# An MoE layer with four experts of 32 slots at a time instead of two of 64, gate and up weights loaded by quarters of the contraction

## The reference, cut to what matters

```python
g_idx = jnp.argmax(g_logits, axis=-1)                 # one group of four
e_val, e_idx = lax.top_k(e_in_group, TOP_K_IN_GROUP)  # two of its eight experts
combine = jnp.sum(jax.nn.one_hot(expert_id, N_EXPERTS) * e_w[..., None], axis=1)
a = jnp.einsum('nd,edh->neh', t, w_gate)
b = jnp.einsum('nd,edh->neh', t, w_up)
act = jax.nn.silu(a) * b * combine[:, :, None]
out = jnp.einsum('neh,ehd->nd', act, w_down)
```

## Time and profile before

| | us |
|---|---|
| median of 3 runs (lowest, highest) | 1275.25 (1270.68, 1278.07) |
| the profiled execution | 1280.37 |
| its span | 1278.5 |
| experts of layer 0: first `gate_up` to end of the last `down` | 314.9 to 626.5 |
| experts of layer 1: first transposes of a round to end of the last `down` | 969.8 to 1239.2 |

### The profile page before, as it was taken

The page is one execution under the profiler, slowest core; times in us unless marked ns, Lnnn a source line. Parts: engine busy times, 40 slices in busy tenths (PEclk is TensorE's granted clock), DMA queues, the critical chain, the costliest instruction groups (busy, mean ns, idle before and its releaser), DMA issues.

```text
span 1278.5 us, 14637 instructions
## 1 busy us (share of the span) xinstructions
PE 1089.1 (85%) x5429; PEld 574.4 (45%) x5429; DVE 476.8 (37%) x1014; ACT 257.0 (20%) x498; POOL 185.4 (15%) x209
## 2 busy tenths in 40 slices
PE   5799888987999789999879999989765988878864
PEld 3344555555444234443345565658662422222223
DVE  3355556234233113332263336784540111111116
ACT  2211334022333123223231110000221000000001
POOL 1020000002322023221100002130011222222100
PEclk8899989986999899999889999999967989889997
DMA  9996985532899569999870200505320899999943
GB/s 351 404 322 264 251 294 225 227 132 70 313 395 401 228 238 356 398 406 410 305 286 1 99 1 0 230 1 198 154 94 20 325 413 413 413 412 407 407 161 129
DMA packets 94241, 324.54 MB, mean 254 GB/s; under 512 B 17647, under 2 KB 33423, under 8 KB 77380
## 3 DMA queue, kind: packets, MB, share of 16 engines
q1 hardware_dynamic: 71936, 303.49, 61.3%
q0 software_dynamic: 15504, 13.37, 3.4%
q10 hardware_dynamic: 6708, 6.45, 1.4%
HBM read 333.22 MB, written 30.11 MB: 284 GB/s over the span
## 4 chain that ended last, share of the span: by engine, by line
PE 63%; DMA 19%; DVE 7%; issue 4%; ACT 3%; SPq 3%; POOL 0%; ACTq 0%; another core or an unknown queue 0%; POOLq 0%; DVEq 0%
PE bank L849 15%; DMA ring<-in_moe_w_up 10%; PE bank L997 10%; PE bank L863 6%; PE bank L668 3%; PE bank L1036 3%; PE bank L784 3%; DMA ring<-in_w_ada 3%; DMA hT<-in_hy_log_decay 3%; PE bank L564 3%; PE bank L599 2%; PE bank L1025 2%; PE bank L983 2%; DMA ring<-in_moe_w_down 2%; PE bank L796 2%
## 5 line engine op out<-in xcount | busy, mean ns | idle before, releaser
L849 PE MATMUL bank<-ring,work 128*64 128x512 f32 x1120 | 267.5, 633 | 44.3 <-issue 38.2
L849 PEld LDWEIGHTS bank<-ring,work 128*64 128x64 f32 x1120 | 82.5, 145 | 220.6 <-issue 216.4
L863 PE MATMUL bank<-ring,work 128*64 128x512 f32 x560 | 129.4, 604 | 4.3 <-DVE work L1643 1.5
L997 PE MATMUL bank<-hT,ring 128*128 128x384 f32 x384 | 128.0, 494 | 5.3 <-ACT hT L1134 5.3
L1655 DVE SCALAR_TENSOR_TENSOR work<-bank,work 128x256 f32<-128x256 f32 x32 | 15.5, 484 | 261.3 <-ACT work L1230 248.6
L997 PEld LDWEIGHTS bank<-hT,ring 128*128 128x128 f32 x384 | 74.0, 194 | 58.0 <-issue 9.7
L863 PEld LDWEIGHTS bank<-ring,work 128*64 128x64 f32 x560 | 37.5, 138 | 74.1 <-issue 63.4
L1230 ACT ACTIVATE work<-bank 128x256 f32<-128x256 f32 x32 | 12.3, 383 | 249.8 <-PE bank L849 249.8
L1667 DVE COPY work<-bank 128x512 f32<-128x512 f32 x32 | 22.1, 692 | 106.8 <-PE bank L863 106.8
L1806 POOL DMA_INDIRECT work<-token_vectors,work x28 | 28.7, 1026 | 199.6 <-PE bank L832 185.7
L564 PE MATMUL bank<-ring,condS 128*32 128x256 f32 x768 | 48.6, 408 | 10.0 <-DVE ada L1334 5.5
(11 more groups left out here) (269 smaller groups left out, 1481.5 us busy)
## 6 DMA issues: line engine op xcount, KB each, us to landing
ring<-in_moe_w_gate SPq DMA_DIRECT2D x32, 2048.0 KB
ring<-in_moe_w_up SPq DMA_DIRECT2D x32, 2048.0 KB
ring<-in_moe_w_down SPq DMA_DIRECT2D x32, 2048.0 KB
ring<-in_w_ada SPq DMA_DIRECT2D x24, 2048.0 KB, 12.5
ring<-in_hy_w_in SPq DMA_DIRECT2D x6, 2048.0 KB, 20.4
filter_spectra<-work ACTq DMA_DIRECT2D x8, 768.0 KB
work<-expert_rows SPq DMA_DIRECT2D x16, 384.0 KB, 6.7
ring<-filter_spectra SPq DMA_DIRECT2D x2, 3072.0 KB, 12.1
```

Source lines behind the costliest of these rows:

```text
L849: last = mm(bank[2][WIN * j:WIN * (j + 1), :], gt[:, k, WIN * j:WIN * (j + 1)], gu[:, :, j, k, :], start=(k == 0), stop=(k == KD - 1))
L863: last = mm(bank[b + hf][WIN * j:WIN * (j + 1), :], AT[:, k, WIN * j:WIN * (j + 1)], dn[:, j, k, hf * HALF:(hf + 1) * HALF], start=(k == 0 ...
L997: last = mm(bank[n % 2][:, 0:T], w[:, k, (n % 4) * P:(n % 4 + 1) * P], hT[:, k, :], start=(k == 0), stop=(k == KD - 1))
```

## The change

The unit becomes a quad: four consecutive experts of 32 slots each (`QUAD` = 4, `WIN` = 32, 8 rounds). `gate_up` is 32 products of 32 slots by 512 columns (64 instructions), four experts in four quarters of the array's columns; `down` is 16 products (32 instructions). Further windows are of 32 slots per expert: up to two per quad are woven into the round (`extra_gate_up` behind the quad's own `gate_up`, `extra_down` behind its `down`), and `rare(q)` takes any beyond two.

A quad's weights fill the whole ring in six units of 2 MB. Units 0 to 3 hold a quarter of the contraction of gate and up for all four experts (two transfers of 1 MB each, contiguous pieces of 2 KB), units 4 and 5 the two halves of down. Units 0 to 3 of the next quad are issued when the activation of this one has been transposed (`at_mm`), so after its further windows' `gate_up` too; units 4 and 5 when the next quad's tokens have been transposed (`gt_mm`), so after `down`.

```diff
-PAIRS = NE // 2
-WIN = 64
+QUAD = 4
+QUADS = NE // QUAD
+WIN = P // QUAD
+WOVEN = 2
...
+        def load_unit(sp, l, q, i):
+
+            if i < 4:
+                cols = slice(i * (KD // 4) * EH, (i + 1) * (KD // 4) * EH)
+                for u, name in enumerate(("moe_w_gate", "moe_w_up")):
+                    src = a[name][l, QUAD * q:QUAD * (q + 1)].rearrange("j (p k) h -> p j (k h)", p=P)
+                    sp.dma_start(part_gu(i)[:, u].rearrange("p j k h -> p j (k h)"), src[:, :, cols])\
+                        .then_inc(sem(f"part_in{i}"), 16)
...
-            for q in range(2, PAIRS):
-                sp.wait_ge(S_("gu_mm"), B_("gu_mm") + q - 1)
-                load_gu(sp, l, q)
-                sp.wait_ge(S_("dn_mm"), B_("dn_mm") + 2 * (q - 1))
-                load_dn(sp, l, q)
-                if l == 0 and q % 2 == 1:
-                    load_filter(sp, q // 2)
+            for q in range(1, QUADS):
+                sp.wait_ge(S_("at_mm"), B_("at_mm") + q)
+                for i in range(4):
+                    load_unit(sp, l, q, i)
+                sp.wait_ge(S_("gt_mm"), B_("gt_mm") + 2 * (q + 1))
+                if l == 0:
+                    load_filter(sp, q)
+                for i in (4, 5):
+                    load_unit(sp, l, q, i)
...
-                for q in range(PAIRS):
-                    s = q % 2
-                    pe.wait_ge(sem(f"gu_in_{s}"), B_("gu_in") + 32 * (q // 2 + 1))
-                    copied(q)
+                for q in range(QUADS):
+                    pe.wait_ge(S_("gta_set"), B_("gta_set") + q + 1)
+                    pe.wait_ge(S_("gtb_set"), B_("gtb_set") + q + 1)
                     if q >= 1:
                         pe.wait_ge(S_("act_set"), B_("act_set") + q)
-                    extra(q)
-                    gate_up(GT, s, S_("gu_mm"))
...
+                    rare(q)
+                    apart(pe)
+                    for i in range(2):
+                        pe.wait_ge(sem(f"part_in{i}"), B_("part_in0") + 32 * (q + 1))
+                        gate_up(GT, i)
+                    if l == 0 and q >= 1:
+                        for part in range(3):
+                            spectra(q - 1, part)
+                    for i in range(2, 4):
+                        pe.wait_ge(sem(f"part_in{i}"), B_("part_in0") + 32 * (q + 1))
+                        last = gate_up(GT, i)
+                    last.then_inc(S_("gu_mm"), 1)
+                    extra_gate_up(q)
                     pe.wait_ge(S_("act_set"), B_("act_set") + q + 1)
-                    turn_act(S_("at_mm"))
...
+                    turn_act(A, S_("at_mm"))
+                    if l == 0:
+                        taps(q, 0)
+                        taps(q, 1)
                     pe.wait_ge(S_("at_set"), B_("at_set") + q + 1)
-                    pe.wait_ge(sem(f"dn_in_{s}"), B_("dn_in") + 16 * (q // 2 + 1))
+                    pe.wait_ge(sem("dn_in"), B_("dn_in") + 32 * (q + 1))
                     if q >= 1:
                         pe.wait_ge(S_("y_set"), B_("y_set") + 2 * q)
-                    down(s, 4, S_("dn_mm"))
...
+                    for hf in range(2):
+                        down(hf).then_inc(S_("dn_mm"), 1)
+                    if l == 0:
+                        taps(q, 2)
+                    extra_down(q)
+                    if q + 1 < QUADS:
+                        pe.wait_ge(S_("gath"), B_("gath") + 16 * (q + 1))
+                        for half in range(2):
+                            gather_turn(half)
+                    if l == 0 and q >= 1:
+                        sizes(q - 1)
```

More of the change, by code:

```diff
@@ L326, in build @@
         mtmp = [small(2, TC, NE) for _ in range(3)]
-        posk, rowk, wck, basek, wink, rowq = [small(2, TC) for _ in range(6)]
+        posk, rowk, wck, basek, wink = [small(2, TC) for _ in range(5)]
         idx = sb("idx", [P, TC * 2], I32)
@@ new lines, in gate_up_all, with turn_act, down @@
+                def gate_up_all(gt):
+                    for i in range(4):
+                        last = gate_up(gt, i)
+                    return last
+                def turn_act(act, done):
+                    for k in range(2):
+                        last = tr(bank[3][:, k * P:(k + 1) * P], act[:, k * P:(k + 1) * P], ident)
+                    last.then_inc(done, 1)
+                def down(hf):
+                    for k in range(2):
+                        for j in range(QUAD):
+                            last = mm(bank[4 + hf][WIN * j:WIN * (j + 1), :], AT[:, k, WIN * j:WIN * (j + 1)],
+                                      unit_dn(k)[:, j, hf * HALF:(hf + 1) * HALF], start=(k == 0), stop=(k == 1))
+                    return last
@@ L1650, in moe @@
                 dve.wait_ge(S_("tab_in"), B_("tab_in") + 16)
[L1651 to L1653 removed]
+                for q in range(QUADS):
+                    rare(q)
+                    apart(dve)
+                    if l == 0 and q >= 1:
+                        spectra(q - 1)
                     dve.wait_ge(S_("silu"), B_("silu") + q + 1)
[L1655 to L1656 removed]
+                    weighted(A, slot_weight(0, q)).then_inc(S_("act_set"), 1)
+                    extra_act(q)
+                    apart(dve)
@@ new lines, in moe @@
+                for q in range(QUADS):
+                    rare(q)
+                    extra_gather(q)
+                    apart(pool)
+                    if q + 1 < QUADS:
+                        if q >= 1:
+                            pool.wait_ge(S_("gt_mm"), B_("gt_mm") + 2 * (q + 1))
+                        gather(G, record(0, q + 1, 1), S_("gath"))
+                    if l == 0 and q >= 1:
+                        size_sums(q - 1)
+                    pool.wait_ge(S_("y_set"), B_("y_set") + 2 * (q + 1))
+                    scatter(Y, record(0, q, 0), S_("scat"))
+                    extra_scatter(q)
+                    apart(pool)
```

607 lines of the change are left out of this document (338 added, 269 removed).

## The result

The changed kernel takes 1320.5 us (median of 4 runs, 1316.4 to 1323.1) against 1276.2 for the kernel before beside it: ratio 1.035, 95% interval 1.031 to 1.039. It is 44 us slower; the forecast was 8 slower, and its range ended at 1304.

A forecast was written before the change was run, and what follows sets the result against it. It took transfers to bound layer 1, and both transfers and TensorE to be near their limit in layer 0. Layer 1 +8, layer 0 -7 and checks +7 gave +8 us on 1275.25: 1283 us, range 1263 to 1304.

The forecast's parts named there:

- the checks term: Checks for further windows on TensorE and ScalarE: a quarter of 28 us exposed, 7 us more in all.
- a sign of being wrong: The prediction would be wrong if layer 0 ended later than before, or TensorE showed long issue gaps before quarters.
- Gaps: Idle DMA time behind quads with further windows: 14 to 16.4 us latency, 12.2 covered; 14 us summed in layer 1.
- Layer 1, stream: Layer 1's weight transfers from 991.9 us: 1227.3 without gaps, 1241.3 with them; last `down` at 1247, layer +8 us.
- the same sum in layer 0: Layer 0's transfers 259 us and gaps 27 us, ending at 619.4 against 626.5: -7 us.
- Pieces: Gate and up weights in 2 KB pieces move at 393 GB/s instead of 411: 6.6 us more per layer.
- The rival of 350 GB/s: Slow pieces or small transfers: each layer loses 18 us more than forecast, 1320 us; chance 0.06.
- Four column parts: A quad's `gate_up` 7.1 us, `down` 3.65, as a pair's; rival: 1.3 times that, 1325 us, chance 0.06.
- Layer 1, start: First load of layer 1 after three windows at 991.9 us, 3 us earlier than before.
- Slower: The changed kernel is slower than before: chance 0.48, from 0.36 for the forecast itself and 0.06 for each of two rivals.
- the likeliest case: The forecast itself: +8 us, 1283 us, slower through gaps behind further windows, pieces and checks; chance 0.36.
- The faster rival: 2 KB pieces run at 411 GB/s and checks are hidden: 1263 us; chance 0.27.

The follow-up runs named there:

- checks only: The changed kernel with the number of further windows set to zero for every quad, all their checks still taken: 1239.7 us.
- run 1: The changed kernel with GpSimd's gather of a quad's further windows issued ahead of the previous quad's scatters: 1309.7 us.
- Run 14: The kernel with gathers ahead; SyncE reads the counts and loads the next quad's weights once the last gate and up products used them: 1289.5 us.
- Run 15: The kernel with gathers ahead, release in the last product, and further windows' transposes and copies ahead of the third quarter's products: 1285.6 us.
- run 18: The kernel of halves with counts read once per quad and the rare check nested, on TensorE, ScalarE and VectorE: 1261.0 us, ratio 0.9911 to the kernel before.
- runs 3 and 4: The changed kernel and the kernel before, each without further windows and without their checks: 1228.3 and 1212.0 us.
- runs 3 to 6: Changed kernel and kernel before, without further windows and their checks: 1228.3 and 1212.0 us; with the checks alone: 1239.7 and 1224.0.
- runs 1 and 9: The second is the kernel with gathers ahead, with down's loads issued only when the quad's third quarter has landed: 1309.9 us; the first was 1309.7.
- run 10: The kernel with gathers ahead, each 1 MB gate or up transfer holding one whole expert, multiplied as it lands in one column part: 1471.2 us.
- run 16: The kernel with gathers ahead, release in the last product and transposes ahead, with gate and up loaded by halves in 2 MB transfers, 4 KB pieces: 1281.6 us.

## Why the prediction was wrong

**The stages.** On the profiled execution (1288.4 forecast, 1323.1 measured) layer 0 was to end at 619.4 and ended at 641.6: 22 us. Layer 1's last `down` was to end at 1247 and did at 1263.9 less layer 0's shift: 17. The tail is 2 longer, and the 7 of the checks term were not in these stages' sums. Without their gaps the two sums were also 6 us short each: 277.5 and 241.1 us, where "checks only" has 283.3 and 247.7. Layer 0 was forecast 7 us earlier than before and ended 15.1 later, which the prediction had named as a sign of being wrong.

**The step that failed is "Gaps"** in "Layer 1, stream", and the same sum in layer 0. It said: 14 to 16.4 us from the last landing to the first byte of the next load, "covered by the down transfers (4.19/0.411 = 10.2) and the rows (0.8/0.411 = 2): 12.2. Gap 2 to 4 us, I take 3.3". It had 14 us of gaps in layer 1 behind `at_mm` of quad 0; "checks only" against the changed kernel gives 30 (247.7 against 277.8 from that load to the end). In layer 0 it had 27; measured 46 (283.3 against 329.5 from first `gate_up` to end). The forecast's 41 us of gaps were 76. Three things were in it; runs 1 and 14, which act on the first two, give back 31 us together:

- *A chain of GpSimd's that I left out.* The scatter of a quad's last further window is waited for before the next quad's further gather is issued, and I costed that gather at 3.5 us from the earlier trace rows, where the queue was empty. Behind a full queue of weights each takes 6.6 to 8.0 us. Run 1 prices it: 11 us, the slower products behind the wait included, which I had at 7.1 us. The Trainium skill has a fit for a transfer issued from GpSimd, some 2 us and its bytes at 436 GB/s (DMA: Bandwidth & Descriptors, Anatomy of one DMA — SWDGE (gpsimd) path); an estimate from it is 2.3 us for the 0.15 MB that moved in the earlier trace rows, where 3.5 was measured, and the gathers behind a full queue are further off still: here the measurement decides.
- *The cover.* 13 us from landing to issue was right. The engines had 8 us of work behind the last quarter in place of 12.2. I had put all of down's 4.19 MB and 0.8 MB of rows behind the landing; 1.1 MB of down and 0.6 of rows had moved before it. So 5 us and the time to the first bytes were open where the sum had 2 to 4, and quads 2 and 3 of run 1 are 6.5 us above "checks only". Run 14, which asks for the weights 5 to 6 us sooner, gives back 20 us in all.
- *The serial work of a round with further windows.* I sized a gap as transfers against one latency and took TensorE's round as the smaller one, except behind quad 0 and in quad 4. Run 15's chain, and run 18's 21 us behind it, show that with the weights there in time the round is TensorE's and its helpers' own.

**Pieces: right.** 393 GB/s forecast by the row at 646 us, 392 and 394 measured beside 411 and 413. The term was 13 us for both layers; runs 3 and 4 differ by 16.3, which holds everything else of the change too. The rival of 350 GB/s is refuted; that its 1320 us is the time measured is coincidence. The Trainium skill's 341 GB/s (DMA: Bandwidth & Descriptors, Bandwidth) is for a transfer of 1 MB alone, and as a price for queued ones the trace doesn't bear it out.

**Four column parts: right.** 7.07 us for 64 woven instructions against 7.09 for 32 in two parts, so a quad costs what a pair did. That rival is refuted. The figure of the Trainium skill behind it (TensorE: Matmul & The Clock Gate, Measured speedup vs the span model: three column tiles 2.38 times one) compares with one tile alone. So measured, four are worth 3.2 here, and two 32 x 0.353/7.09 = 1.6, an estimate, as no run has 64 slots in one part. The loss is there, but all of it already in the pair's row, and the forecast weighed it against that row, which was the wrong comparison.

**Layer 1, start: 6 us better than forecast.** The first load was to come at 991.9 and came at 1002.2, which is 986.1 without the shift of 16.1 from layer 0.

**Checks: 7 us forecast.** With no further windows they make no difference between the two kernels (11.4 and 12.0). Where TensorE bounds the rounds, the reads are worth 21 (run 18).

**The direction.** "Slower" had 0.48 and was right; the likeliest case had the right sign, by gaps and pieces, but the rounds with further windows got 41 us of gaps (27 and 14) where 76 (46 and 30) were lost. The faster rival wanted pieces at no cost, which didn't hold, and checks hidden, which came out as no difference between the kernels in runs 3 to 6.

## What to carry to other kernels

A kernel that streams weights and releases them only after its rarest extra work should be costed round by round, once for the transfers and once as the serial chain of every engine that the extra work visits, with its queue's small transfers at their price behind a full queue. Running both kernels without the extra work splits a difference into base and extra, and it is worth doing before any repair. A busy share that falls (85 to 77% here) promises nothing: work was taken from where the transfers covered it, and waits were put where nothing did.

## What was unexpected of the hardware

- A small indirect transfer from GpSimd takes 3.5 us with the weights' queue empty and 6.6 to 8.0 if it is issued behind a full one (layer 0 and 1 of the changed kernel).
- When the landing of a quad's last quarter is seen, 1.1 MB of the `down` asked for behind it on the same queue have moved, in runs 1 and 9 alike.
- 64 instructions of 32 slots by 512 columns take 22.57 us if a column part does its 16 in a row, and 7.07 if the four take turns (run 10).
- With gate and up in pieces of 2, 4 and 8 KB, full queues move 384 to 394, 405 and 411 to 422 GB/s.
- Issuing 1 MB in 2 KB pieces holds SyncE for 0.4 to 0.5 us at the start of a quad's loads and mostly for about 2.5 us or more, up to 7.3, once some are queued; with 8 KB pieces at most 2.4. No run shows that this delays a transfer.
- The 4.89 us of issue at 1027.36 in run 18 coincide with a packet on the instruction queue between 1022 and 1028; there is none between 988 and 992, where the same place takes 1.61. In run 16 the place takes 4.91 and 4.93 us with such a packet and 2.96 without. That instructions are loaded at a branch there was not tested and stays open.
